# Four of the eight head pairs keep their token-wise tiles on the other half of the partitions, and a prologue with fewer angle steps

## What is computed

```python
sk    = state @ kk_t
state = state * w_t - outer(sk, kk_t * a_t) + outer(v_t, k_t)
y_t   = state @ r_t          # then a norm over the head, a bonus term, a gate, and @ w_out
```

## Time and profile before

| | |
|---|---|
| profiled execution | 2938.78 us |
| span, first to last instruction | 2937.0 us |
| TensorE busy (PE) | 2683.2 us, 91% |
| VectorE busy (DVE) | 1589.4 us, 54% |
| GpSimd busy (POOL) | 1246.0 us, 42% |
| ScalarE busy (ACT) | 948.4 us, 32% |
| mean granted TensorE clock | 0.974 of full |
| recurrence | about 1634 to 2112 us |

### The profile page before, as it was taken

The page is one execution under the profiler, slowest core; times in us unless marked ns, Lnnn a source line. Parts: engine busy times, 40 slices in busy tenths (PEclk is TensorE's granted clock), DMA queues, the critical chain, the costliest instruction groups (busy, mean ns, idle before and its releaser), DMA issues. The chain is left out here.

```text
span 2937.0 us, 51498 instructions
## 1 busy us (share of the span) xinstructions
PE 2683.2 (91%) x21600; PEld 2204.9 (75%) x21600; DVE 1589.4 (54%) x2030; ACT 948.4 (32%) x1615; POOL 1246.0 (42%) x630
## 2 busy tenths in 40 slices
PE   1878888999999999989999599999799999999999
PEld 1565667788887788767777488888787888788887
DVE  5754454665553633366865478888435333333334
ACT  2434433322214222244544233343334222222221
POOL 2532224544435444444344335444356444444443
PEclk9989999999999999999999899999999999999999
DMA  6421224345442222237566444444232222223223
GB/s 242 154 93 37 86 83 154 128 174 172 165 136 86 94 100 101 94 102 187 156 172 158 115 97 98 95 95 87 89 122 86 101 97 97 87 93 108 94 100 122
DMA packets 299013, 341.94 MB, mean 116 GB/s; under 512 B 214560, under 2 KB 214688, under 8 KB 298784
## 3 DMA queue, kind: packets, MB, share of 16 engines
q1 hardware_dynamic: 298784, 338.65, 37.3%
HBM read 297.77 MB, written 39.85 MB: 115 GB/s over the span
## 5 line engine op out<-in xcount | busy, mean ns | idle before, releaser
L709 POOL TENSOR_TENSOR wl<-w,wh 128x1024 fp32r<-128x1024 f32 x367 | 902.3, 2465 | 1278.6 <-ACT wh L750 1278.3
L180 PE MATMUL ps<-hi,wh 128*128 128x512 f32 x2208 | 884.6, 401 | 21.7 <-ACT qk_raw L787 10.0
L181 PE MATMUL ps<-lo,wh 128*128 128x512 f32 x2208 | 869.8, 394 | 0.0
L182 PE MATMUL ps<-hi,wl 128*128 128x512 f32 x2208 | 869.3, 394 | 0.0
L750 ACT ACTIVATE wh<-w 128x1024 fp32r<-128x1024 f32 x367 | 386.9, 1056 | 684.3 <-DMA w<-in_ffn_w_in 523.0
L1021 DVE SCALAR_TENSOR_TENSOR xt<-ps,mod,xt 128x512 f32<-128x512 f32 x384 | 286.4, 749 | 425.2 <-PE ps L182 417.8
L180 PEld LDWEIGHTS ps<-hi,wh 128*128 128x128 f32 x2208 | 420.9, 191 | 124.9 <-issue 33.6
L181 PEld LDWEIGHTS ps<-lo,wh 128*128 128x128 f32 x2208 | 421.4, 191 | 90.3 <-issue 3.7
L182 PEld LDWEIGHTS ps<-hi,wl 128*128 128x128 f32 x2208 | 420.2, 190 | 90.2
L1026 DVE TENSOR_TENSOR act<-ps,silu 128x512 f32<-128x512 f32 x88 | 60.8, 691 | 482.2 <-PE ps L182 482.2
L180 PE MATMUL ps<-act_hi,wh 128*128 128x512 f32 x704 | 282.3, 401 | 16.4 <-DVE act_lo L1030 9.7
(11 more groups left out here) (225 smaller groups left out, 3443.2 us busy)
## 6 DMA issues: line engine op xcount, KB each, us to landing
w<-in_ffn_w_in SPq DMA_DIRECT2D x176, 512.0 KB, 3.3
piece<-in_ada_w SPq DMA_DIRECT2D x96, 512.0 KB, 5.0
w<-in_ffn_w_out SPq DMA_DIRECT2D x88, 512.0 KB, 3.3
w<-in_w_rkv SPq DMA_DIRECT2D x48, 512.0 KB, 3.8
scratch<-silu SPq DMA_DIRECT2D x48, 256.0 KB, 3.0
scratch<-act SPq DMA_DIRECT2D x48, 256.0 KB, 2.8
w<-in_wqk SPq DMA_DIRECT2D x20, 512.0 KB, 4.7
xt<-in_xT SPq DMA_DIRECT2D x4, 2048.0 KB, 11.8
```

The source lines that it names most:

```text
L180: pe.matmul(out, w_hi(k), x_hi(k), start=first and k == 0, stop=False)
L181: pe.matmul(out, w_hi(k), x_lo(k), start=False, stop=False)
L182: ins = pe.matmul(out, w_lo(k), x_hi(k), start=False, stop=last and k == kc - 1)
L709: pool.tensor_tensor(wl[n % NW][:, :, :], wr[n % NW][:, :, :], wh[n % NW][:, :, :].bitcast(F32), ALU.subtract).then_inc(*wlo.up)
```

## The change

In the recurrence, tiles that are indexed by token keep the heads of pairs 4 to 7 on the other half of the partitions ("away"), and tiles that are indexed by feature, and the inverse's right-hand factor, stay ("home"). A product that goes from one kind to the other then reads one half and writes the other for pairs 4 to 7, and the order of heads takes pairs i and i+4 next to each other, so that consecutive products go to the four 64x64 parts of the array. Pairs 4 to 7 write their own PSUM bank (`two_banks`, `spot`). Products from home to home (the second product of each `level_t`, the product with the state in `solve_x` and in the outputs, `by_feature`) keep the diagonal parts. `solve_x` is cut in two: `known_x`, ahead of `by_feature`, and the product with the state, behind it. `outputs` and `state_products` become one function that also takes over `chunk_used`. The levels' DVE adds and ACT copies go from two halves to one instruction of 512 columns. On DVE `new_state` goes ahead of `centre`. The blocks that `tdiag_t` loads come as four DMAs in place of two.

In the prologue the cosine is made from the sine's reduced angle (ACT computes the sine of half pi minus its absolute value), so the second reduction goes and one DVE instruction comes. SP no longer loads weight tiles at the first ada part; it loads three at piece step 12, and the second half of x directly behind them.

```diff
 # SP, prologue
-                            if step == "part" and e[1] == 0:
+                            if step == "part" and e[1] == 0 and tiles[e[0]][0] == "ada" and tiles[e[0]][-1] == 1:
+                                pass
+                            elif step == "part" and e[1] == 0:
                                 load(top[e[0]] + AHEAD + 1)
                             elif step == "piece":
                                 load_pieces(e[0] + (3 if e[1] != 3 else min(3, KC - 1 - e[2])))
-                                if e[0] == 13:
-                                    sp.dma_start(xt[:, :, half[1]], t["xT"][:, :, half[1]]).then_inc(*x_in[1].up)
                                 if e[0] == 12:
                                     load(AHEAD)
+                                    sp.dma_start(xt[:, :, half[1]], t["xT"][:, :, half[1]]).then_inc(*x_in[1].up)
 # DVE, angles
-                            for j, quarter in enumerate((0.0, 0.25)):
-                                after(dve.tensor_scalar(turns, ang, 1.0 / TWO_PI, quarter, ALU.mult, ALU.add))
-                                after(dve.tensor_scalar(turns, turns, ROUND, None, ALU.add))
-                                after(dve.tensor_scalar(turns, turns, ROUND, None, ALU.subtract))
-                                if j == 1:
-                                    dve.wait_ge(*trig_done.at(1))
-                                after(dve.scalar_tensor_tensor(red, turns, -PI_A, ang, ALU.mult, ALU.add))
-                                for part in (PI_B, PI_C):
-                                    after(dve.scalar_tensor_tensor(red, turns, -part, red, ALU.mult, ALU.add))
-                                after(dve.tensor_scalar(red, red, quarter * TWO_PI, ANG_MAX, ALU.add, ALU.min))
-                                dve.tensor_scalar(red, red, -ANG_MAX, None, ALU.max).then_inc(*red_done.up)
+                            after(dve.tensor_scalar(turns, ang, 1.0 / TWO_PI, ROUND, ALU.mult, ALU.add))
+                            after(dve.tensor_scalar(turns, turns, ROUND, None, ALU.subtract))
+                            after(dve.scalar_tensor_tensor(red, turns, -PI_A, ang, ALU.mult, ALU.add))
+                            for part in (PI_B, PI_C):
+                                after(dve.scalar_tensor_tensor(red, turns, -part, red, ALU.mult, ALU.add))
+                            dve.tensor_scalar(red, red, ANG_MAX, -ANG_MAX, ALU.min, ALU.max).then_inc(*red_done.up)
+                            dve.wait_ge(*red_done.at(1))
+                            dve.scalar_tensor_tensor(turns, red, -1.0, red, ALU.mult, ALU.max).then_inc(*red_done.up)
 # recurrence: where a head's tile lies, and the order of heads
+                def spot(b, j, half, off=0):
+                    return ps[half, b + j // QP, off + j % QP * CHUNK:off + (j % QP + 1) * CHUNK]
+                def home(j, h):
+                    return slice(h * HEAD, (h + 1) * HEAD)
+                def away(j, h):
+                    return home(j, h if j < QP else 1 - h)
+                def heads(pairs=PAIRS):
+                    for i in range(pairs // 2):
+                        for j in (i, i + pairs // 2):
+                            for h in range(2):
+                                yield j, home(j, h), away(j, h)
 # PE, serial part
+                        def known_x(ch):
+                            pe.wait_ge(*g["k_out"].at(min(ch + 3, NC)))
+                            pe.wait_ge(*g["g_out"].at(ch + 1))
+                            pe.wait_ge(*g["s_step"].at(ch))
+                            pe.wait_ge(*g["yc_done"].at(ch))
+                            for j, to, hs in heads():
+                                ins = pe.matmul(spot(3, j, to), gk[b][hs, j, 0, :], vtok[ch % (RING + 1)][hs, j, :], start=j % QP == 0, stop=False)
+                        def solve_x(ch):
+                            pe.wait_ge(*g["s_done"].at(ch))
+                            for j, hs, _ in heads():
+                                ins = pe.matmul(spot(3, j, hs), ar[ch % (RING + 1)][hs, j, 0, :], state[hs, j, :], start=False, stop=j % QP == QP - 1)
+                        def outputs_and_state(ch):
+                            pe.wait_ge(*g["ue_done"].at(ch + 1))
+                            pe.wait_ge(*g["yc_done"].at(ch))
+                            for j, to, hs in heads():
                                pe.matmul(spot(3, j, to, HALF // 2), gk[b][hs, j, 1, :], vtok[ch % (RING + 1)][hs, j, :], start=j % QP == 0, stop=False)
...
                            for j, to, hs in heads():
                                ins = pe.matmul(spot(3, j, to), btok[b][hs, j, :], ust[hs, j, :], start=False, stop=False)
                            ins.then_inc(*g["y_known"].up)
 ...
 # by_token, n == 1
+                                pe.wait_ge(*g["yc_done"].at(max(ch - 2, 0)))
 # PE, period
-                                solve_x(zz)
+                                known_x(zz)
                             if zp is not None:
                                 by_feature(zp)
+                            if zz is not None:
+                                solve_x(zz)
...
 # DVE, period
-                                level(y, 1, 0), level(y, 1, 1)
+                                level(y, 1)
                             if zz is not None:
-                                centre(zz)
+                                new_state(zz), centre(zz)
                             if x is not None:
-                                products_b(x)
-                            if zz is not None:
-                                new_state(zz)
-                            if x is not None:
-                                decayed_keys(x)
+                                products_b(x), decayed_keys(x)
```

More of the change, by code:

```diff
@@ new lines, in level_t @@
+                            pe.wait_ge(*g["w_done"].at(NL * ch + l + 1))
+                            pe.wait_ge(*g["t_done"].at(NT * ch + 2 * l))
+                            if l == 0:
+                                pe.wait_ge(*tt_in[ch % 2].at(4 * (ch // 2 + 1)))
+                            if l < NL - 1:
+                                for j, hs, to in heads():
+                                    ins = pe.matmul(spot(0, j, to), old[hs, j, :], wx[l % 2][hs, j, :], start=True, stop=True)
@@ L1665, in solve_x @@
                             pe.wait_ge(*g["g_out"].at(ch + 1))
-                            for j, hs in heads(0, PAIRS):
-                                pe.matmul(bank(6)[hs, j, :], gk[b][hs, j, 0, :], vtok[ch % (RING + 1)][hs, j, :], start=True, stop=False)
-                                ins = pe.matmul(bank(6)[hs, j, :], ar[ch % (RING + 1)][hs, j, 0, :], state[hs, j, :], start=False, stop=True)
+                            pe.wait_ge(*g["s_step"].at(ch))
+                            pe.wait_ge(*g["yc_done"].at(ch))
@@ new lines, in outputs_and_state @@
+                            for j, to, hs in heads():
+                                pe.matmul(spot(3, j, to), ktok[b][hs, j, :], vtok[ch % (RING + 1)][hs, j, :], start=False, stop=False)
+                            for j, to, hs in heads():
+                                pe.matmul(spot(3, j, to, HALF // 2), arb[b][hs, j, :], ust[hs, j, :], start=False, stop=False)
+                            for j, to, hs in heads():
+                                ins = pe.matmul(spot(3, j, to), btok[b][hs, j, :], ust[hs, j, :], start=False, stop=False)
@@ new lines, in outputs_and_state @@
+                            ins.then_inc(*g["y_known"].up)
+                            for j, hs, _ in heads():
+                                if j < QP:
+                                    pe.matmul(spot(3, j, hs, HALF // 2), ar[ch % (RING + 1)][hs, j, 1, :], state[hs, j, :], start=False, stop=j % QP == QP - 1)
+                            pe.wait_ge(*g["y_known"].at(ch + 1))
+                            for j, hs, _ in heads():
+                                if j >= QP:
+                                    ins = pe.matmul(spot(3, j, hs, HALF // 2), ar[ch % (RING + 1)][hs, j, 1, :], state[hs, j, :], start=False, stop=j % QP == QP - 1)
@@ L1904, in period @@
                             if y is not None:
[L1905 removed]
+                                level(y, 0)
                             if d is not None:
```

152 lines of the change are left out of this document (64 added, 88 removed).

## The result

The changed kernel takes **2958.32 us**, median of five runs (2951.74 to 2959.53), against 2944.93 for the kernel before on the same chip. The ratio is **1.0053, 95% interval [1.0031, 1.0074]**: some 15 us slower. The forecast was 2914. The profiled execution took 2951.74 (span 2950.0) against 2938.78 (2937.0).

The account below looks back on a forecast made before the run. PE was taken as the bound, DVE 3 us behind. Against 2938.8: prologue -17.5, periods -5.5, drain -4, filling -2, clock +4 sum to -25, hence 2914; own range 2903 to 2925, 8 in 10 for 2896 to 2938.

Parts of the forecast that it names:

- The feed: PE's four-part products: instructions fed at 7 ns each, 14 a pair, so 0.5 us a group in place of 0.93.
- outputs: Recurrence period: u at B+8.7 (B: line 1759), then four groups, state product and tail, ending at B+11.55; -0.25 us.
- Rival 1: Small products on PE fed no faster than 27 ns a record, 0.86 a group; period 28.7, total 2955; chance 7%.
- The common end: DVE's `new_state` moved ahead of `centre`: +0.6 us a period for its multiply beside POOL, bounds 0 and +1.1.
- The clock: Full periods: PE's busy share falls to about 65%, a third of 12 periods meet a clock drop; +4 us, bounds 0 and +20.
- at the end: Drain, last three intervals: groups on the serial chain save 0.43 each, `new_state` before `centre` costs 1.3; -4 us.
- The prologue: Before the first product: shorter angles and later weight tiles, sixteenth piece at about 49; -17.5 us, bounds -13 and -21.
- rival 4: Prologue's gain is given back to POOL contention or later pieces; half stays, 2923 to 2930; chance 12%.
- ahead of `y_norm`: DVE in each recurrence period: still waits 1.7 us at `y_norm`, which comes at B+24.1 against 24.55 (B: line 1759).
- a contended multiply: DVE in the recurrence: `new_state`'s multiply, 0.69 us before, would take 1.2 to 1.3 beside POOL.
- the filling: First intervals of the recurrence, where DVE waits for level products and outputs: -2 us.
- signs of being wrong: Whole forecast: wrong if periods are above 26.3 us or the first product is later than 60.

Follow-up runs that it names:

- One_end_before: Kernel before with the changed prologue, plus only the changed dependence: state's products directly behind outputs, DVE waits for both, `new_state` ahead of `centre`; ratio 1.0050.
- two_ends: Changed kernel with y in banks 5 and 6 and done before the state; `centre` waits for y alone, ahead of `new_state`; first gram behind `level_t` 1; ratio 1.0036.
- two_ends_root: two_ends with ScalarE's root and next squares ahead of the last level's copy; ratio 0.9997 to the kernel before.
- root_first_after: Changed kernel with ScalarE's root and next squares ahead of the last level's copy; ratio 1.0014 to the kernel before.
- prologue_only: Kernel before with only the changed prologue (angles, `load`, second half of x); ratio 0.9957, 12.6 us less.

## Why the prediction was wrong

**The feed: the step that failed.** The forecast read the feed from 64 instructions in 0.4 us behind an idle gap and called it 7 ns an instruction. The groups did run at 0.47, but that pace lasts for one block: in the long run the feed gives 14.5 ns, and the old groups with their 29 ns a pair (0.93/32) ran just at it. In a row of such groups four tiles can only bring the next stop forward. This bound is one of stretches, not of the whole period: before and after the change PE fetched 62 packets in the 11 full periods, 5.6 a period, and at 3.75 us each these are 21 us of 26.3 or 27.9. The forecast's step "outputs" shows it term by term, in the period above: u was there at B+8.9 (forecast 8.7), the groups took 0.47, yet the state came at B+14.6 and not at 11.55, with 2.6 us of it in two stops (2034.61 to 2035.63, and 2037.49 to 2039.10 where the state's products should have begun). This period, the first of the draining, has more of it than most. In the mean of the 11 full periods u is there at B+9.0 and the state at B+13.75, 2.2 us late, of which PE's stops behind u are 1.4. From the state to the next B it is 14.1 us, where the forecast had 14.3. So the whole excess of the period (27.85 against 25.85) lies ahead of the state, and some two thirds of it are stops. The small terms were off too: by its own row and its own +0.1 the forecast's u was at B+8.9, not 8.7, and the first level add came at B+4.96, where it had about 4.5. Rival 1 named a limit of the stream, and its total (2955) is near the measured one, but partly by luck: its period of 28.7 is 0.85 too long and its prologue gains 7 us too much. Its form was wrong: not 27 ns on each record, but starts 14.6 ns apart and then a stop. I gave it 7%.

**The common end.** The forecast moved `new_state` ahead of `centre` at a price of 0.6 for contention. That both now wait for five groups instead of three had no price of its own: at 0.5 a group the five end ahead of the old B+11.80, at 0.93 they would end 1.7 us later than at 0.5. One_end_before measures the dependence, in the old recurrence, at 27 us. In the forecast four-tile groups were to pay for it, and without their pace nothing did. In the changed kernel, taking it out again gave back only 5 us (two_ends against the changed kernel, and two_ends_root against root_first_after), so the costs do not simply add up.

**The clock.** +4 was forecast for the full periods; they ran at 0.97. A large miss is at the end, where +13 came for -4. Windows of 20 us in the drain, after and before:

```profile
2092.00:2112.00 20.00, 12.41 (x331) 11.60 (x320) 5.51 (x9) 3.07 (x8) 3.54 (x3) 0.66 0.01 3
```
```profile
2079.00:2099.00 20.00, 18.06 (x580) 17.51 (x576) 7.87 (x16) 4.53 (x12) 3.53 (x3) 1.00 0.12 40
```

The clock is at 1.2 GHz for most of it. In the changed kernel's PE timeline four-tile groups there start 0.85 apart (2104.38, 2105.23, 2106.08), with a granted clock of 0.50. PE had more and longer waits than before the change, and DVE waits 8.93 us for the last chunk's state:

```profile
2108.85 0.69 DVE L1896 TENSOR_TENSOR state<-ps,state 128x512 f32<-128x512 f32 x1 [8.93 <-PE ps L1719]
```

Not all of these 13 us are the clock: one_end_before, with two-tile products, takes 85.7 in this stretch against prologue_only's 78.4, so the dependence alone can make about 7 of them. The rest is not parted.

**The prologue** gave 10.7 of 17.5. That it frees the queues was right (their share in 23 to 37 is 0.66, was 0.00). The sixteenth piece ends at 52.5 and not at 49 (+3.5); the forecast's own terms, twelve pieces of 1.6 behind 32, give 51.2. From its end to the first product it is 10.0 us instead of 6.5 (+3.5), the splits beside the two multiplies: I had the splits "under the 7.9 us that follow anyway" and forgot that they are not free for DVE. Of the 10.7 us 1.6 went back by the start of the recurrence, and prologue_only kept its gain to the end, so rival 4 did not happen.

**What held:** groups at 0.47 to 0.5, 0.93 on the diagonal, 1.71 ahead of `y_norm`, a contended multiply (1.63, forecast 1.2 to 1.3, but its median over twelve periods is 0.92), and the filling, which was better than said. Both of the prediction's signs of being wrong came true: periods above 26.3 and a first product later than 60.

**What stays open.** The old recurrence with its best order takes 25.8 a period, the changed one with two ends and the same exchange 27.6. The runs don't split these 1.8 us, nor the +15.6 of the change, between stops, clock and the coarser steps (whole levels in place of halves); no version of the changed kernel ran at the old 0.93 a group, since even the pairs in order overlap.

## What to carry to other kernels

Before speeding up many small products, count PE's instructions per period against 3.7 us for 256: a burst measured over 64 instructions says nothing of the stream. An average below that pace is no safety either, since the stops fall where instructions come densely; look for idle time put down to "issue" at even counts of instructions. And look first at each engine's order for a step that stands behind a copy it does not need: here that one exchange brought 8.5 to 11 us, and no version with the four-tile layout came under the old recurrence with the same prologue (0.9957).

## What the runs showed of the hardware

- PE takes 256 instructions in 1.9 us with four tiles of 64 columns and then stands, 3.75 us from block to block, with the transfer queues otherwise idle. With 128 columns four tiles halve the time (28.5 against 55.7 ns a pair), without a stop to speak of.
- Products whose order uses two tiles for eight products and then the other two still overlap at the seams: 0.59 us a group, between 0.47 and 0.93.
- The same period of the same kernel takes 24.5 or 28.8 us, with the granted clock at 1.00 or 0.89 (two_ends_root; the waits differ too, so this is not the price of the clock alone).
